# Two-layer hybrid block on one core: four reorderings inside the mixing stage and one at the end of the program

## The chip, the cores and the metric

One Trainium2 chip, one of its NeuronCores. The metric is device time in microseconds from launch to finish of one execution, median of several. The engines are named as in the profile: PE (TensorE) multiplies matrices, DVE (VectorE), ACT (ScalarE) and POOL (GpSimd) work element by element, SP issues DMAs. All inputs are float32 in HBM.

## The reference

Two layers over a 256 x 1024 activation `x`, each a feed-forward block, a mixing block with three branches, a cross attention to a memory and another feed-forward block:

```
for l in range(DEPTH):                                   # 2
    x = x + 0.5 * swiglu_ffn(rms_norm(x, ffn1_norm[l]), ffn1_w_gu[l], ffn1_w_down[l])
    h = rms_norm(x, mix_norm[l])
    (x_r, g_r, q_b, c_kv, q_i, k_i, w_i, q_c, k_c, v_c, f_c,
     gate_a, gate_b, gate_c) = jnp.split(h @ w_in[l], _split_points(), axis=-1)
    o_a = rglru_branch(...)      # convolution, two gates, a scan over time
    o_b = dsa_branch(...)        # 8 index heads score the keys, top 64 kept, softmax over them
    o_c = fox_branch(...)        # causal softmax with a forget bias
    merged = (sigmoid(gate_a) * (o_a @ w_branch[l, 0]) + sigmoid(gate_b) * (o_b @ w_branch[l, 1])
              + sigmoid(gate_c) * (o_c @ w_branch[l, 2]))
    x = x + merged @ w_out[l]
    x = x + memory_cross_attention(rms_norm(x, xattn_norm[l]), rms_norm(mem, mem_norm[l]), ...)
    x = x + 0.5 * swiglu_ffn(rms_norm(x, ffn2_norm[l]), ffn2_w_gu[l], ffn2_w_down[l])
return rms_norm(x, final_norm)
```

## The kernel before

**Weights.** Every weight comes through a ring of three SBUF slots in units of 1 MB (`raw`, 128 x 2048). To multiply in `float32r` without losing precision, ACT copies a unit, rounded, to `w_hi` in two halves (`split_hi`, L535) and DVE writes the rest `w_lo = raw - w_hi`, again in two halves (`split_lo`, L543). PE then forms three products per unit: hi x hi, hi x lo, lo x hi. A unit's split is written three units ahead of its use; the call is `splits(..., name)`, which splits the unit that takes the slot of `name`.

**Order.** There is no scheduler. Each engine's program is written out by hand, and engines wait for one another on semaphores that count: `job_done` (PE has finished a group), `bank_free[b]` (the result in bank b of `work` was taken away), `hi_ready`, `lo_ready`, `lg_ready`, `exp_ready`, `ri_ready`, `p_ready`. Class `Plan` walks through the units and groups in PE's order; `job` gives each group one of the four banks of `work` in turn, with two exceptions. A group may start only when the bank's previous group has been evacuated.

**The mixing stage** of a layer runs in this order on PE: normalized `x` through transposes (`nt`), units `xr0` to `gr1` of the first branch, the unit `misc` (whose result `nat` holds the key of the index, the latent `c` and the forget logits), the gates `rg` 0 and 1, transposes `fT` and `ki`, unit `qi0`, gates 2 and 3, transpose `cT`, unit `qi1`. Then the **index part**: eight small groups `("dots", i)`, with a unit after each second one (`qc0`, `kc0`, `qc1`, `kc1`). ACT takes relu of each (L1057), DVE sums them into `score` (`index_scores`). DVE does `index_scores(7)` only after the first logits.

Then the **stream**, 19 slots s with one unit each (`FILL`: `vc0`, `vc1`, `qb0`, `qb1`, `ga0`, ... `gc2` in slot 13, `gc3` 14, `bc1` 15, `gb0` 16). Softmax k (16 of them: 8 for the third branch, 8 for the second) passes through all engines: PE logits `("qk", k)` into `acc`; DVE scales and adds the bias into `lg[k % 2]` and takes the extreme (`nm`, `lg_ready`); ACT takes exp with sums (L1087, `exp_ready`); DVE the reciprocal (L1476, `ri_ready`); POOL multiplies (L797, `p_ready`); in slot k + 1 PE transposes the result (`("pt", k)`, L1920), and ACT copies it to `pt`. PE forms the logits 0 at the start of slot 0 and those of 2m - 1 and 2m at the start of odd slots.

DVE's program in a slot s is: logits of s; the first half of the split; reciprocal of s; `o_lo` of a finished pair; gating; the second half of the split; then, in slots 0 to 7, two of the sixteen top-8 rounds (two pairs of `max` and `match_replace`, L1496 and L1498) on `score`; in slots 13 to 16 the low part of two tiles of the normalized memory, `mem_lo` (`norm_lo`, L1184), which frees the bank of `("mt", s - 13)`. PE writes that bank with four transposes (L1938) just after the `pt` of the slot. The second branch's bias (`t5_score`, POOL) of softmax 8 to 11 needs the top 64 of rows 0 to 127 (rounds of slots 0 to 3), that of 12 to 15 those of rows 128 to 255 (slots 4 to 7).

**The end.** The last unit's product comes in four blocks of 128 x 512 (`LAST_BLOCKS`). For each DVE adds the block to `x` (`residual`, L1198) and multiplies by the final gain (L1205); ACT takes squares (L820), POOL the power -1/2 of the sums, and ACT and DVE each scale one half of a row block into `final_out`, which SP stores.

## Time and profile before

| | |
|---|---|
| runs | 1366.32 us median of 3 (1364.59 to 1366.35) |
| profiled execution | 1366.55 us, span 1364.7 us from first to last instruction |
| PE busy | 1344.5 us, 99% of the span |
| DVE busy | 951.2 us, 70% |
| ACT busy | 790.0 us, 58% |
| POOL busy | 133.8 us, 10% |
| granted clock of PE | 0.999 on average |

A timeline row gives the start, the duration and the number of like instructions in a row; in brackets stands the idle time of the engine before the row and what released it. PE's ends are modelled: groups that follow one another directly overlap a little by their rows, so that starts are the better measure there. The two layers repeat the same pattern some 674 us apart. The mixing stage lies at 195 to 500 us in layer 0 and at 869 to 1175 us in layer 1.

### The profile page before, as it was taken

Reading aid. Unit: us, or ns where it says so; the run is one execution under the profiler, and the core shown is the slowest. Engines: PE = TensorE matmul, PEld = TensorE weight load, DVE = VectorE, ACT = ScalarE, POOL = GpSimd, SP = SyncE. Lnnn points to the kernel's source line nnn. Section 1 sums busy time; section 2 is a strip of 40 time slices with the busy share of each in tenths; the row PEclk is TensorE's granted clock in tenths of the full one; section 3 lists DMA queues with packets and bytes.
Section 4 is the critical chain, followed back from the end, with each engine's and each line's share of the span. In section 5 each row is a group of like instructions: output and inputs, shape, how many; then the busy total and the mean of one; then the engine's idle time right before and its main releaser. Section 6 shows DMA issues by size and latency. Waiting matters only on the chain.

```text
span 1364.7 us, 23703 instructions
## 1 busy us (share of the span) xinstructions
PE 1344.5 (99%) x8805; PEld 1205.6 (88%) x8805; DVE 951.2 (70%) x1460; ACT 790.0 (58%) x1405; POOL 133.8 (10%) x168
## 2 busy tenths in 40 slices
PE   8999999999999999999999999999999999999997
PEld 7888889999999988888888888899999989888886
DVE  6666678888756667666676666789877656666665
ACT  7555566755744565555565555686566446655554
POOL 4010010022400110000010000101233001100000
PEclk9999999999999999999999999999999999999999
DMA  8687655655545447666566667555454555476661
GB/s 264 200 205 214 196 157 178 202 162 163 155 157 194 146 129 213 193 198 189 170 190 196 184 184 211 149 186 185 142 192 132 171 170 167 143 211 189 184 187 76
DMA packets 286385, 243.39 MB, mean 178 GB/s; under 512 B 14344, under 2 KB 263608, under 8 KB 286304
## 3 DMA queue, kind: packets, MB, share of 16 engines
q1 hardware_dynamic: 284176, 236.77, 57.1%
q10 hardware_dynamic: 1600, 4.25, 1.0%
q0 software_dynamic: 528, 1.26, 0.6%
q8 instruction: 54, 0.88, 0.3%
q14 instruction: 27, 0.22, 0.0%
HBM read 241.18 MB, written 1.27 MB: 178 GB/s over the span
## 4 chain that ended last, share of the span: by engine, by line
PE 60%; issue 24%; DVE 8%; ACT 4%; DVEq 3%; POOL 1%; POOLq 1%; ACTq 0%
PE work L1738 18%; PE acc L1695 16%; PE work L1666 12%; PE work L1742 9%; DVE w_lo L543 3%; PE work L1679 2%; ACT w_hi L535 1%; DVEq L1425 1%; PE acc L1591 1%; DVE score L1424 1%; ACT lg L1087 1%; POOL lg L797 1%; PE work L1908 1%; PE work L1920 1%; POOLq L742 0%
## 5 line engine op out<-in xcount | busy, mean ns | idle before, releaser
L543 DVE TENSOR_TENSOR w_lo<-raw,w_hi 128x1024 fp32r<-128x1024 f32 x444 | 543.1, 1244 | 89.7 <-ACT w_hi L535 87.9
L535 ACT ACTIVATE w_hi<-raw 128x1024 fp32r<-128x1024 f32 (+1 forms) x442 | 450.5, 1052 | 26.0 <-PE acc L1695 25.4
L1738 PE MATMUL work<-act,w_hi 128*128 128x512 f32 x1408 | 440.2, 394 | 0.0
L1742 PEld LDWEIGHTS work<-act,w_lo 128*128 128x128 f32 x1408 | 264.7, 188 | 60.2
L1742 PE MATMUL work<-act,w_lo 128*128 128x256 f32 x1408 | 277.7, 279 | 0.0
L1738 PEld LDWEIGHTS work<-act,w_hi 128*128 128x128 f32 x1408 | 214.7, 188 | 3.3 <-issue 0.2
L1666 PE MATMUL work<-act,w_hi 128*128 128x256 f32 x1536 | 197.9, 282 | 2.7 <-ACT act L995 1.1
L1666 PEld LDWEIGHTS work<-act,w_hi 128*128 128x128 f32 x1536 | 184.9, 188 | 8.0 <-issue 2.6
L851 ACT ACTIVATE gu_s<-work 128x256 f32<-128x256 f32 x176 | 57.8, 380 | 182.9 <-PE work L1742 182.9
L1219 DVE TENSOR_TENSOR gu_s<-gu_s,work 128x256 f32<-128x256 f32 x176 | 66.1, 417 | 121.7 <-ACT gu_s L851 121.3
L1695 PE MATMUL acc<-w_hi,h_lo 128*128 128x512 f32 x320 | 126.0, 394 | 0.0
L1695 PE MATMUL acc<-w_lo,h_hi 128*128 128x512 f32 x320 | 125.4, 392 | 0.0
L1695 PE MATMUL acc<-w_hi,h_hi 128*128 128x512 f32 x320 | 124.2, 388 | 0.0
L739 POOL TENSOR_SCALAR ms<-ssq 128x1 f32<-128x1 f32 x22 | 20.2, 916 | 883.8 <-ACT junk L820 883.1
L1666 PE MATMUL work<-act,w_lo 128*128 128x256 f32 x768 | 97.0, 278 | 0.0
L1666 PEld LDWEIGHTS work<-act,w_lo 128*128 128x128 f32 x768 | 92.3, 188 | 0.0
L861 ACT ACTIVATE h_hi<-h_f 128x256 fp32r<-128x256 f32 x80 | 33.4, 418 | 98.6 <-PE acc L1695 82.8
L1695 PEld LDWEIGHTS acc<-w_lo,h_hi 128*128 128x128 f32 x320 | 60.1, 188 | 12.3
L1695 PEld LDWEIGHTS acc<-w_hi,h_lo 128*128 128x128 f32 x320 | 60.2, 188 | 11.9
L1695 PEld LDWEIGHTS acc<-w_hi,h_hi 128*128 128x128 f32 x320 | 60.1, 188 | 11.8
L1238 DVE TENSOR_TENSOR h_lo<-h_f,h_hi 128x256 fp32r<-128x256 f32 x80 | 33.8, 422 | 45.7 <-ACT h_hi L861 45.7
L797 POOL TENSOR_TENSOR lg<-lg,ri 128x256 f32<-128x256 f32 (+1 forms) x32 | 39.1, 1222 | 195.1 <-DVE ri L1476 195.1
(247 smaller groups left out, 1541.7 us busy)
## 6 DMA issues: line engine op xcount, KB each, us to landing
raw<-in_ffn_w_gu SPq DMA_DIRECT2D x174, 512.0 KB, 5.0
raw<-in_w_in SPq DMA_DIRECT2D x52, 1024.0 KB, 5.2
raw<-in_ffn_w_down SPq DMA_DIRECT2D x44, 1024.0 KB, 4.9
raw<-in_w_branch SPq DMA_DIRECT2D x12, 1024.0 KB, 5.1
raw<-in_w_mkv SPq DMA_DIRECT2D x8, 1024.0 KB, 5.3
raw<-in_w_out SPq DMA_DIRECT2D x8, 1024.0 KB, 4.9
raw<-in_w_mq SPq DMA_DIRECT2D x4, 1024.0 KB, 5.4
raw<-in_w_mo SPq DMA_DIRECT2D x4, 1024.0 KB, 5.0
```

The lines of the kernel that those rows point to most:

```text
L535: eng.activation(halves(w_hi, slot, kind, part), halves(raw, slot, kind, part), ACT.Copy)\
L543: eng.tensor_tensor(halves(w_lo, slot, kind, part), halves(raw, slot, kind, part), halves(w_hi, slot, kind, part).bitcast(F32), ALU.subtra ...
L797: g.tensor_tensor(lg[:, s % 2, :, 0:s_len], lg[:, s % 2, :, 0:s_len], ri[:, s % 2, :].unsqueeze(2).to_broadcast([P, 2, s_len]), ALU.mult)\
L851: a.activation(gu_s[:, c, g, :], work[:, 2 * c + g, SEQ:2 * SEQ], ACT.Copy).then_inc(cross_ready, 1)
L861: a.activation(dst[:, c, :], h_f[:, c, :], ACT.Copy).then_inc(h_hi_ready, 1)
L1219: v.tensor_tensor(gu_s[:, c, g, :], gu_s[:, c, g, :], work[:, 2 * c + g, 0:SEQ], ALU.add)\
L1238: v.tensor_tensor(lo[:, c, :], h_f[:, c, :], hi[:, c, :].bitcast(F32), ALU.subtract)\
L1666: mm = pe.matmul(ps2(job)[:, m, :], ww[:, slot, first:first + P], xx[:, k, :], start=(n == 0 and k == 0 and m == 0), stop=(n == 2 and k == ...
L1679: mm = pe.matmul(out_ps(tt), xx[:, k, tt * P:tt * P + P], ww[:, slot, k * 256 + cols[0]:k * 256 + cols[1]], start=(n == 0 and k == 0 and t ...
L1695: mm = pe.matmul(acc[:, tt, nh * 512:nh * 512 + 512], xx[:, k0 + kk, tt * P:tt * P + P], ww[:, slot, kk * D + nh * 512:kk * D + nh * 512 + ...
L1738: pe.matmul(work[:, 2 * c + g, :], w_hi[:, slot, at_w:at_w + P], act[:, :, k, :], start=(k == 0), stop=False, skip_group_check=True)
L1742: mm = pe.matmul(work[:, 2 * c + g, 0:SEQ], w_lo[:, slot, at_w:at_w + P], act_hi[:, k, :], start=False, stop=(k == KT - 1), skip_group_che ...
```

## The change

1. **First norm of the mixing stage (DVE).** `scaled_rows(0)` and `(1)` (each scales a pair of transposed tiles in `acc`, 0.69 us) stand ahead of `scaled_xr(0)`.
2. **ACT before the index part.** The gates `rg` 0 ahead of the two squares of the latent, and the copy of `cT` ahead of the gates 2 and 3 and of the split `qi0`.
3. **First logits.** PE forms `("qk", 0)` ahead of the unit `kc1`, not behind it. ACT takes the first exp ahead of the copy of `kc1` and of the split that follows it. DVE takes the reciprocal ahead of that split's first half.
4. **Top-8 rounds.** Slots 0 to 5, 7 and 8 instead of 0 to 7: slot 6 has none.
5. **Banks.** `gc2` and `mt` 1 exchange banks 2 and 0; `mt` 3 and `gb0` exchange 0 and 1.
6. **`mem_lo`** ahead of the second half of the split in slots 13 to 16.
7. **The end.** DVE adds block 3 to `x` straight after block 2, before it multiplies block 2 by the gain and scales row block 0. ACT takes all four squares before it scales row block 0.

```diff
+TOP_SLOTS = (0, 1, 2, 3, 4, 5, 7, 8)
+SWAPPED = {("bc1", 1): 1, ("pt", 15): 3, "gc2": 2, ("mt", 1): 2, ("mt", 3): 1, "gb0": 3}
...
-            if name in (("bc1", 1), ("pt", 15)):
-                bank = (bank + (1 if name[0] == "bc1" else 3)) % 4
+            bank = (bank + SWAPPED.get(name, 0)) % 4
...
                 wait_done(a, l, "nat")
...
+                rg_gates(0)
                 a.drain()
                 for tt in range(TT):
                     a.activation(c_nat[:, tt, :], nat[:, tt, HD + HEADS:F_AT], ACT.Square,
                                  accum_out=ssq[:, tt, 0:1]).then_inc(ssq_ready, 1)
-                rg_gates(0)
...
+                copy_out(l, "cT", c_t[:], ps("cT")[:, 0:SEQ])
                 rg_gates(2)
                 rg_gates(3)
...
                 splits(a, split_hi, l, "qi0")
-                copy_out(l, "cT", c_t[:], ps("cT")[:, 0:SEQ])
...
+                    if i == IDX_SLOTS - 1:
+                        exponential(0)
                     if i in IDX_FILL:
                         filler(l, IDX_FILL[i])
                         splits(a, split_hi, l, IDX_FILL[i])
...
-            squares(DEPTH, 0, range(3))
+            squares(DEPTH, 0)
             for tt in range(TT):
-                if tt == 1:
-                    squares(DEPTH, 0, (3,))
...
-                scaled_xr(0)
                 scaled_rows(0)
                 scaled_rows(1)
+                scaled_xr(0)
...
                     if s == 0:
                         index_scores(IDX_SLOTS - 1)
+                        reciprocals(s)
                     ahead = FILL[s - 1] if s else IDX_FILL[IDX_SLOTS - 1]
                     splits(v, split_lo, l, ahead, (0,))
...
                     filler(l, FILL[s], (0,))
+                    if 13 <= s < 17:
+                        for k in (2 * (s - 13), 2 * (s - 13) + 1):
+                            norm_lo(l, 4, k, mem_hi, mem_lo, ("mt", k // 2), 3)
                     splits(v, split_lo, l, ahead, (1,))
...
-                    if s < 8:
+                    if s in TOP_SLOTS:
+                        at_s = TOP_SLOTS.index(s)
...
+                    for b in range(2):
+                        residual(l, 3, None, (b,))
+                        gained_block(b)
+                    residual(l, 3, None, (2, 3))
                     final_scale(0)
-                    residual(l, 3, None, (3,))
+                    gained_block(2)
+                    gained_block(3)
                     final_scale(1)
...
                     mm.then_inc(job_done, 1)
+                    if i == IDX_SLOTS - 1:
+                        qk(0)
                     if i in IDX_FILL:
                         filler(l, IDX_FILL[i])
```

**ACT at the border of index part and stream.** The rows begin with the relu of `dots` 7; `lg,sm<-lg,nm` is the first exp, `kc<-work` the copy of `kc1`, `w_hi<-raw` the split behind it. Before:

```order
L1057 ACTIVATE lg<-work 128x512 [waits score_step,job_done]
L844 ACTIVATE kc<-work 128x512 [waits job_done]
L535 ACTIVATE w_hi<-raw 128x1024 [waits job_done,landed1]
L535 ACTIVATE w_hi<-raw 128x1024
L1087 ACT_TABLE_LOAD
L1087 ACTIVATE lg,sm<-lg,nm 128x128 [waits lg_ready]
L1087 ACTIVATE lg,sm<-lg,nm 128x128
```

Now:

```order
L1069 ACTIVATE lg<-work 128x512 [waits score_step,job_done]
L1059 ACT_TABLE_LOAD
L1059 ACTIVATE lg,sm<-lg,nm 128x128 [waits lg_ready]
L1059 ACTIVATE lg,sm<-lg,nm 128x128
L847 ACTIVATE kc<-work 128x512 [waits job_done]
L538 ACTIVATE w_hi<-raw 128x1024 [waits job_done,landed1]
L538 ACTIVATE w_hi<-raw 128x1024
```

The table load and the two exps have moved over the copy and the split, which now stand behind a wait for `lg_ready`.

**DVE at the end of slot 6 and in slot 7.** The first row is the second gating of `ba0` (`merged<-gate,work`), which ends slot 6 but for the rounds; `lg<-acc,fox_bias` is the logits of slot 7, and what follows it belongs to that slot. Before:

```order
L1291 SCALAR_TENSOR_TENSOR merged<-gate,work 128x512 [waits bank_free0,job_done]
L1496 MAX top_134<-score 128x8
L1498 MATCH_REPLACE score<-top_134,score 128x256
L1496 MAX top_134<-score 128x8
L1498 MATCH_REPLACE score<-top_134,score 128x256
L1457 SCALAR_TENSOR_TENSOR lg<-acc,fox_bias 128x512 [waits causal_ready,job_done]
L1469 TENSOR_REDUCE nm<-lg 128x2
L543 TENSOR_TENSOR w_lo<-raw,w_hi 128x1024 [waits hi_ready]
L1476 RECIPROCAL ri<-sm 128x2 [waits exp_ready]
```

Now:

```order
L1292 SCALAR_TENSOR_TENSOR merged<-gate,work 128x512 [waits bank_free0,job_done]
L1462 SCALAR_TENSOR_TENSOR lg<-acc,fox_bias 128x512 [waits causal_ready,job_done]
L1474 TENSOR_REDUCE nm<-lg 128x2
L546 TENSOR_TENSOR w_lo<-raw,w_hi 128x1024 [waits hi_ready]
L1449 RECIPROCAL ri<-sm 128x2 [waits exp_ready]
L1487 TENSOR_TENSOR o_lo_72<-work,o_hi_71 128x2x128 [waits o_part]
L546 TENSOR_TENSOR w_lo<-raw,w_hi 128x1024 [waits hi_ready]
L1505 MAX top_134<-score 128x8
L1507 MATCH_REPLACE score<-top_134,score 128x256
```

The four rows of rounds between slot 6 and slot 7 are gone. Slot 7 keeps its rounds, and the last four rows of rounds now stand in slot 8.

**DVE in slot 15.** `gate<-gate,work` and `merged<-merged,gate` are the first gating of `bc1`, `mem_lo` the low part of memory tiles 4 and 5. Before:

```order
L1295 SCALAR_TENSOR_TENSOR gate<-gate,work 128x512 [waits bank_free2,job_done]
L1298 TENSOR_TENSOR merged<-merged,gate 128x512
L543 TENSOR_TENSOR w_lo<-raw,w_hi 128x1024 [waits hi_ready]
L1184 SCALAR_TENSOR_TENSOR mem_lo<-work,gain,mem_hi 128x256 [waits act_hi_ready]
L1184 SCALAR_TENSOR_TENSOR mem_lo<-work,gain,mem_hi 128x256
L1295 SCALAR_TENSOR_TENSOR gate<-gate,work 128x512 [waits bank_free1,job_done]
L1298 TENSOR_TENSOR merged<-merged,gate 128x512
```

Now:

```order
L1296 SCALAR_TENSOR_TENSOR gate<-gate,work 128x512 [waits bank_free0,job_done]
L1299 TENSOR_TENSOR merged<-merged,gate 128x512
L1191 SCALAR_TENSOR_TENSOR mem_lo<-work,gain,mem_hi 128x256 [waits act_hi_ready]
L1191 SCALAR_TENSOR_TENSOR mem_lo<-work,gain,mem_hi 128x256
L546 TENSOR_TENSOR w_lo<-raw,w_hi 128x1024 [waits hi_ready]
L1296 SCALAR_TENSOR_TENSOR gate<-gate,work 128x512 [waits bank_free1,job_done]
L1299 TENSOR_TENSOR merged<-merged,gate 128x512
```

`mem_lo` and the half split have changed places; the bank that the gate row waits for is 0 instead of 2.

## Rows read from the trace of the kernel before

**Rows 1.** Page, section 1: busy us (share of the span) x instructions.
```profile
PE 1344.5 (99%) x8805; PEld 1205.6 (88%) x8805; DVE 951.2 (70%) x1460; ACT 790.0 (58%) x1405; POOL 133.8 (10%) x168
```

**Rows 2.** Waits of PE: line, waited for; us in total, times, longest.
```profile
PE work L1920 <- POOL lg L797: 3.1, 4, 0.8
PE work L1938 <- DVE mem_lo L1184: 1.9, 2, 0.9
PE work L1666 <- ACT act L995: 1.1, 2, 0.5
PE work L1666 <- ACT c_t L844: 0.9, 2, 0.6
```

**Rows 3.** Windows: us; busy PE, PEld, DVE, ACT, POOL; PEclk, DMA, GB/s.
```profile
241.30:278.90 37.60, 36.40 (x311) 34.27 (x310) 34.30 (x55) 27.32 (x41) 3.03 (x2) 1.00 0.64 199
1357.50:1361.00 3.50, 0.00 (x0) 0.00 (x0) 2.20 (x5) 1.67 (x6) 0.86 (x2) 1.00 0.39 150
```

**Rows 4.** Timeline, DVE, slot 0: start, duration in us, engine, line, operation.
```profile
272.01 0.42 DVE L1469 TENSOR_REDUCE nm<-lg 128x2 f32<-128x256 f32 x1
274.05 1.23 DVE L543 TENSOR_TENSOR w_lo<-raw,w_hi 128x1024 fp32r<-128x1024 f32 x1 [0.17 <-issue]
...
275.27 1.21 DVE L543 TENSOR_TENSOR w_lo<-raw,w_hi 128x1024 fp32r<-128x1024 f32 x1
```

**Rows 5.** Timeline, ACT, slot 0, layer 0.
```profile
269.79 2.00 ACT L535 ACTIVATE w_hi<-raw 128x1024 fp32r<-128x1024 f32 x2
271.80 1.28 ACT L1087 ACT_TABLE_LOAD   x1
273.10 0.40 ACT L1087 ACTIVATE lg<-lg,nm 128x128 f32<-128x128 f32 x1
```

**Rows 6.** Timeline, POOL and PE, slots 1, 2; brackets: idle, releaser.
```profile
280.80 1.51 POOL L797 TENSOR_TENSOR lg<-lg,ri 128x256 f32<-128x256 f32 x1 [3.85 <-DVE ri L1476]
...
277.00 0.44 PE L1920 MATMUL work<-ident,lg 128*128 128x128 f32 x2 [0.83 <-POOL lg L797]
...
282.93 0.38 PE L1920 MATMUL work<-ident,lg 128*128 128x128 f32 x2
```

**Rows 7.** Timeline, DVE, ACT and PE, slots 6 to 8, layer 0.
```profile
320.14 0.41 DVE L1496 MAX8 top<-score 128x8 f32<-128x256 f32 x1
...
322.32 0.69 DVE L1457 SCALAR_TENSOR_TENSOR lg<-acc,fox_bias 128x512 f32<-128x512 f32 x1
...
323.81 0.51 ACT L1087 ACTIVATE lg<-lg,nm 128x256 f32<-128x256 f32 x1 [1.19 <-DVE nm L1469]
...
321.75 1.98 PE L1666 MATMUL work<-act,w_lo 128*128 128x256 f32 x16
323.57 1.98 PE L1666 MATMUL work<-act,w_hi 128*128 128x256 f32 x16
326.28 0.66 PE L1920 MATMUL work<-ident,lg 128*128 128x128 f32 x4 [0.74 <-POOL lg L797]
```

**Rows 8.** Timeline, slot 13 (ACT, PE) and 16 (DVE, PE), layer 0.
```profile
362.74 0.60 ACT L844 ACTIVATE pt<-work 128x512 f32<-128x512 f32 x1 [0.19 <-PE work L1920]
...
363.33 0.74 PE L1666 MATMUL work<-act,w_hi 128*128 128x256 f32 x4 [0.20 <-DVE gate L1295]
...
384.30 0.87 DVE L1184 SCALAR_TENSOR_TENSOR mem_lo<-work,gain,mem_hi 128x256 fp32r<-128x256 f32 x2
...
385.31 0.63 PE L1938 MATMUL work<-ident,mem_x 128*128 128x128 f32 x4 [0.94 <-DVE mem_lo L1184]
```

**Rows 9.** Timeline, PE and DVE, end of the program.
```profile
1356.99 0.40 PE L1695 MATMUL acc<-w_hi,last_lo 128*128 128x512 f32 x1
...
1358.22 0.74 DVE L1198 SCALAR_TENSOR_TENSOR x<-acc,scaled_rstd,x 128x512 f32<-128x512 f32 x1
```

**Rows 10.** Timeline, PE, start of the program.
```profile
3.69 2.61 PE L1801 MATMUL work<-ident 128*128 128x128 f32 x11 [3.69 <-POOLq L733]
...
9.80 1.91 PE L1801 MATMUL work<-ident 128*128 128x128 f32 x16
```

More of the change, by code:

```diff
@@ L1050, in _, with exponential @@
                 splits(a, split_hi, l, "qi1")
+                def exponential(s):
+                    s_len = P * ((s % 8) // 4 + 1)
+                    a.wait_ge(lg_ready, l * STREAM + s + 1)
+                    for j in range(2):
+                        e = a.activation(lg[:, s % 2, j, 0:s_len], lg[:, s % 2, j, 0:s_len], ACT.Exp, scale=-1.0,
+                                         bias=nm[:, s % 2, j:j + 1], accum_out=sm[:, s % 2, j:j + 1])
+                    e.then_inc(exp_ready, 1)
                 for i in range(IDX_SLOTS):
@@ L1082, in _ @@
                         splits(a, split_hi, l, FILL[s - 1])
-                    if s < STREAM:
-                        s_len = P * ((s % 8) // 4 + 1)
-                        a.wait_ge(lg_ready, l * STREAM + s + 1)
-                        for j in range(2):
-                            e = a.activation(lg[:, s % 2, j, 0:s_len], lg[:, s % 2, j, 0:s_len], ACT.Exp, scale=-1.0,
-                                             bias=nm[:, s % 2, j:j + 1], accum_out=sm[:, s % 2, j:j + 1])
-                        e.then_inc(exp_ready, 1)
+                    if 0 < s < STREAM:
+                        exponential(s)
                     if s in (2, 3):
@@ L1444, in _, with reciprocals @@
                         splits(v, split_lo, l, IDX_FILL[i])
+                def reciprocals(s):
+                    v.wait_ge(exp_ready, l * STREAM + s + 1)
+                    v.reciprocal(ri[:, s % 2, :], sm[:, s % 2, :]).then_inc(ri_ready, 1)
                 for s in range(STREAM + 3):
@@ L1499, in _ @@
                             v.drain()
-                        if s % 4 == 3:
+                        if at_s % 4 == 3:
                             v.tensor_scalar(sc, sc, 0.5 * TAKEN, NEG, ALU.is_gt, ALU.mult).then_inc(score_ready, 1)
-                    if 13 <= s < 17:
-                        for k in (2 * (s - 13), 2 * (s - 13) + 1):
-                            norm_lo(l, 4, k, mem_hi, mem_lo, ("mt", k // 2), 3)
                     if s != 6:
@@ L1574, in final_scale, with gained_block @@
                                         ALU.mult).then_inc(out_ready[1], 1)
-                    residual(l, 3, None, range(3))
+                    def gained_block(b):
+                        tt, nh = LAST_BLOCKS[b]
+                        cols = slice(nh * 512, nh * 512 + 512)
+                        if b == 0:
+                            v.wait_ge(final_gain_landed, 16)
+                        v.drain()
+                        v.tensor_tensor(final_out[:, tt, cols], x[:, tt, cols], final_gain[:, cols], ALU.mult)\
+                         .then_inc(gained, 1)
+                    for b in range(2):
+                        residual(l, 3, None, (b,))
+                        gained_block(b)
+                    residual(l, 3, None, (2, 3))
                     final_scale(0)
-                    residual(l, 3, None, (3,))
+                    gained_block(2)
+                    gained_block(3)
                     final_scale(1)
@@ L1833, in _, with qk @@
                 late_transposes(l, 1, params)
+                def qk(k):
+                    blk, pr = slot_of(k)
+                    s_len = P * (blk + 1)
+                    queries, keys = (qc, kc) if k < 8 else (qb, k_b)
+                    wait_jobs(pe, l, [f"qc{pr // 2}", f"kc{pr // 2}"] if k < 8 else [f"qb{pr // 2}", ("kb", pr // 2)])
+                    if k >= 2:
+                        pe.wait_ge(lg_ready, l * STREAM + k - 1)
+                    for j in range(2):
+                        mm = pe.matmul(logits(k)[:, j, :], queries[HD * j:HD * j + HD, pr, blk * P:blk * P + P],
+                                       keys[HD * j:HD * j + HD, pr, 0:s_len], start=True, stop=True)
+                    mm.then_inc(job_done, 1)
                 def rg_gates(m):
@@ L1889, in _ @@
                     for k in qk_slots(s):
-                        blk, pr = slot_of(k)
-                        s_len = P * (blk + 1)
-                        queries, keys = (qc, kc) if k < 8 else (qb, k_b)
-                        wait_jobs(pe, l, [f"qc{pr // 2}", f"kc{pr // 2}"] if k < 8 else [f"qb{pr // 2}", ("kb", pr // 2)])
-                        if k >= 2:
-                            pe.wait_ge(lg_ready, l * STREAM + k - 1)
-                        for j in range(2):
-                            mm = pe.matmul(logits(k)[:, j, :], queries[HD * j:HD * j + HD, pr, blk * P:blk * P + P],
-                                           keys[HD * j:HD * j + HD, pr, 0:s_len], start=True, stop=True)
-                        mm.then_inc(job_done, 1)
+                        qk(k)
                     if pv_pair(s) is not None:
```

17 lines of the change are left out of this document (6 added, 11 removed).

## Prediction

> **What bounds the kernel now.** I read the page's busy shares first. PE is busy 1344.5 of 1364.7 us [rows 1], so that no reordering can win more than the 20 us in which it isn't, start and end of the program included. The second view is what PE waits for. It holds all that this change can reach: transposes of a softmax waiting for POOL's multiplication, 3.1 us in four waits; the memory transposes waiting for DVE's `mem_lo`, 1.9 us in two; projection units waiting for ACT, 1.1 and 0.9 us in four [rows 2]. Each occurs once or twice a layer. The third view, windows, shows who stands behind these waits. From 241.3 to 278.9 us, the index part up to slot 1, DVE is busy 34.30 of 37.60 us with 55 groups [rows 3]; the 3.3 us left are 0.06 us apiece, the drains between dependent operations. DVE waits for nobody there. That stretch, and not PE, sets when the first softmaxes are done, and the reader should keep it in mind: PE time that is won ahead of it can be lost at its end.
>
> **Part 1 and 2, before the index part.** The waits for `act` (0.55 us a layer) and for `c_t` (0.45) mostly go, since ACT gets its first scaled tiles one DVE piece sooner and copies `cT` before two gates. DVE itself gains at most the few tenths that it waited there for ACT, and ACT hands as much back with the copy, about 0.4 us, that now stands in front of the gates 2 and 3, which release DVE's long stretch. So DVE's stretch begins when it did, within 0.1 us. PE arrives about 1 us sooner at the end of the index part. Value of its own: nothing, if PE is then made to wait for the same DVE stretch (next part).
>
> **Part 3, first logits.** Moving PE's four matmuls costs nothing. What counts is the queue on ACT. DVE reaches `nm` of softmax 0 at 272.01 + 0.42 = 272.43 [rows 4] as before, because DVE and not PE was late there. ACT has had its table load (1.28 us) by then; before, too, it ran at 271.80, ahead of `nm` [rows 5]. The two exps take some 0.9 us (0.40 each and the readouts [rows 5]) and end at 273.4. DVE's reciprocal follows at 274.05, where the half split stood [rows 4], and not at 275.2. Even with 1.51 us for the multiplication [rows 6] `p_ready` comes at 275.8 and not at 276.95: the stall of 0.83 us at 277.00 [rows 6] goes.
>
> But the copy of `kc1` and its split now stand behind ACT's wait. Copy 273.4 to 273.9 (0.60 us for this shape [rows 8], starts overlap by 0.1), first half split to 274.95, second to 275.9 (2.00 us the two [rows 5]). DVE, which took these halves at 274.05 and 275.27 and ended at 276.48 [rows 4], can take the first at 275.0 to 276.2 and the second to 277.3. It is 0.85 us later, and it has no reserve: rounds, logits 1, split and reciprocal follow on one another. POOL's multiplication of softmax 1 ends not at 280.80 + 1.51 = 282.31 but at 283.16, and PE transposes it at 283.2, not at 282.93 [rows 6]. So PE, 1.8 us ahead (0.83 + about 1), waits some 2.1 us in slot 2 and leaves it **0.27 us later than before**. Bounds: below, -1.83 us a layer, if nothing of this holds PE (0.83 + 0.55 + 0.45); above, +1.55, if the table load starts only with `nm` (0.27 + 1.28). I take +0.27, since the rows of slot 0 carry each step. Two layers: **+0.5 us** (-3.7 to +3.1).
>
> **Part 4, rounds.** In slot 7 PE stands 0.74 us before the transposes at 326.28. By starts it is more: the groups at 321.75 and 323.57 are 1.82 apart, so that the next was due at 325.39, 0.89 before [rows 7]. The two rounds of slot 6 fill 320.14 to 322.32, when the logits of slot 7 begin [rows 7]. Without them DVE is 2.1 us sooner, but ACT's exp can use only the 1.19 us that it stood idle (323.81 [rows 7]); its splits come first. 1.15 against 0.89: the stall goes, with 0.25 us to spare. The rounds themselves, 2.2 us, lie in slot 8, where PE has no wait and DVE has the 2.1 us in hand that it got in slot 6. Bounds: 0 to -0.89; the margin would be gone if the multiplication took 0.25 longer, and POOL's spans vary by more than that. I take all: **-1.8 us** for two layers.
>
> **Parts 5 and 6, banks and `mem_lo`.** In slot 16 the transposes `mt` 3 stand 0.94 us, by starts 1.0, until `mem_lo` of `mt` 2 is through at 384.30 + 0.87 [rows 8]. Now `mt` 3 goes to bank 1, which the gating of `bc1` freed before 383, and `mem_lo` is a half split earlier; `gb0`, in bank 0, needs that `mem_lo` only by 384.6, when it is done at 384.1. The wait goes: **-2.0 us** for two layers (bounds 0 and -2.1). In slot 13 `gc2` waited 0.20 us for DVE's gating, to 363.33. In bank 0 it waits for ACT's copy of `pt` 12, 362.74 + 0.60 = 363.34 [rows 8]: no gain. The split halves that fall behind `mem_lo` are needed two slots later.
>
> **Part 7, the end.** PE's last product ends at 1356.99 + 0.40 = 1357.39, and DVE takes it up at 1358.22 [rows 9], 0.8 us late, because it first multiplies block 2 by the gain and scales. Squares, sums, power and last scaling hang on it one after the other. They start 0.8 us sooner; DVE's own queue behind it, two gain products and two scalings, is nearly as long as that chain and takes 0.1 back: **-0.7 us** (0 to -0.8).
>
> **Sum.** +0.5 - 1.8 - 2.0 - 0.7 = -4.0 us; with the rounding of part 3 (0.54) and part 4 (1.78), -3.9. From the profiled execution's 1366.55 that gives 1362.65; the median of the runs is 0.23 lower, so 1362.4.
>
> **Rivals.** (a) *DVE doesn't hold slot 2.* Then parts 1 to 3 give their 1.83 us a layer instead of costing 0.27: 4.2 us more, 1358.2. For it: ACT stands idle there, and its order can matter in ways that rows of the other order don't show. Against it: DVE's 34.30 of 37.60 us.
>
> (b) *ACT comes later still, or slot 7 keeps its wait.* If the table load waits with the exp, DVE loses 1.28 us more in each layer: 1365.0. The same if POOL's multiplication in slot 7 eats the margin (1.8 us back: 1364.2). Against it: the load at 271.80 ran before its operand was there.
>
> (c) *The exchange moves the wait and doesn't remove it.* In bank 2 the pair product of slot 15 now follows `mt` 1, and needs its `mem_lo` earlier than `mt` 2 did. If `mem_lo` of slot 14 were 1 us late there, the 2.0 us would stay: 1364.4. Against it: it no longer stands behind a half split.
>
> (d) *Slower.* The 2.1 us hole in slot 2 is over twice as long as any stall that PE has now. If it made the granted clock fall to the lower of its levels, 1.2 instead of 2.4 GHz, matmuls would run at half pace for a while. The start shows that pace: 11 transposes in 2.61 us at 3.69, 16 in 1.91 at 9.80, and at most 6.1 us between the two [rows 10]. Half of 6.1 in each layer is 6.1 us more: 1368.5. It decides at the hole's length. Against it: after the last matmul PE was idle from 1357.50 to 1361.00 with the granted clock at 1.00 [rows 3], 3.5 us, more than the hole. The Trainium skill (TensorE: Matmul & The Clock Gate, Part 1) says that the gate grants by how busy PE has been recently and that the throttled state is the default; by that rule a hole can cost a stretch at half rate, and the trace agrees only that the clock does fall some time after the work ends, later than this hole would last.
>
> **Chances and range.** Forecast 0.66, (a) 0.08, (b) 0.14, (c) 0.09, (d) 0.03. The range goes from inside (a) to (b), 1358.8 to 1365.2: it leaves out (d) and the far halves of (a) and (b). A measurement of this kernel tells 0.2%, 2.7 us, from no change; the forecast lies 1.2 us beyond that. Faster 0.70: the forecast but for a tenth of its cases, and (a). Same 0.26: (b), (c) and that tenth. Slower 0.04.
>
> **What the profile will show.** Right: PE's waits for `mem_lo` gone; no wait at the first softmax transposes of a stream, and one of about 2 us at the second; none in slot 7; the DVE half split of slot 0 begun near 275 us and waiting for ACT's `w_hi`; last residual 0.04 us after the last matmul. Wrong: stream slot 2 ends sooner than before relative to the layer's start (a); table load after `nm`, or a wait in slot 7 (b); a wait of the pair product on `mem_lo` in slot 15 (c); a granted clock under 1.00 inside the mixing stage (d).

## The result, and the profile after

| | before | after |
|---|---|---|
| median of 5 runs | 1366.06 us (1364.59 to 1366.35) | 1358.49 us (1357.65 to 1359.28) |
| span of the profiled execution | 1364.7 us | 1356.7 us |
| PE busy | 1344.5 us | 1338.8 us |

The ratio is 0.9946 (95% interval 0.9935 to 0.9957): 7.6 us faster, where 3.9 us were forecast. The time lies 0.3 us under the range.

The busy times from the page of after answer [rows 1]:

```profile
PE 1338.8 (99%) x8805; PEld 1202.2 (89%) x8805; DVE 953.3 (70%) x1460; ACT 789.4 (58%) x1405; POOL 127.8 (9%) x168
```

PE executes the same 8805 matmuls and is busy 5.7 us less. About half of that is how busy time is counted: a matmul in front of a wait counts with its modelled end, some 0.28 us, and with 0.11 us where the next one follows directly, so that waits and small matmuls that go or change places take 2.7 us of busy time with them. The other 2.9 us lie between 256-column matmuls that follow one another directly in both kernels. No term of the sum had a place for those.

The waits of PE in after answer [rows 2] (columns: line, waited for; us in total, times, longest):

```profile
PE work L1944 <- POOL lg L800: 4.4, 4, 1.9
PE work L1685 <- ACT pt L847: 0.5, 2, 0.2
PE work L1757 <- DVE w_lo L546: 0.4, 1, 0.4
```

The waits for `mem_lo`, `act`, `c_t` and `gate` are gone. That for POOL's multiplication has grown from 3.1 to 4.4 us: it went from the first softmax of a stream, where 0.33 us are left, to the second. On PE's timeline, layer 0, after, answering [rows 6]:

```profile
274.30 0.44 PE L1944 MATMUL work<-ident,lg 128*128 128x128 f32 x2 [0.33 <-POOL lg L800]
...
278.35 2.05 PE L1698 MATMUL work<-w_hi,act 128*128 128x256 f32 x16
282.29 0.44 PE L1944 MATMUL work<-ident,lg 128*128 128x128 f32 x2 [1.90 <-POOL lg L800]
```

The hole in slot 2 is there, 1.90 us by this view and 2.06 by starts, where 2.1 was forecast.

**Where PE's time went.** I set the start of each matmul in the trace of after against its counterpart of before. The last one starts 7.94 us sooner. The rest of the program, up to the end, is 0.09 us shorter.

| place | forecast, both layers | traces |
|---|---|---|
| start of the program | 0 | -0.15 |
| up to slot 2 (parts 1 to 3) | +0.54 | -0.63 (-0.49 and -0.14) |
| slot 7 (part 4) | -1.78 | -1.79 |
| slot 16 (parts 5, 6) | -2.0 | -2.27 |
| matmuls that follow one another faster | none | -3.1 (what is left) |
| after the last matmul (part 7) | -0.7 | -0.09 |
| sum | -3.9 | -8.0 |

The second line holds some pace of its own, 0.2 us gained in layer 0 and 0.3 us lost in layer 1. By waits and order alone the two layers are alike there, -0.30 and -0.43. The expectations below give 0.54 and 0.20 us for this line; matmul by matmul it is 0.49 and 0.14. "Slot 7" is the prediction's name: it goes by softmax 7, whose transposes PE does in slot 8.

**The pace.** The fifth line can be read off the timeline. Here a row is a group of 16 matmuls, and the difference of two starts is the time of 16. Before, in the first units behind slot 16:

```profile
394.34 2.05 PE L1666 MATMUL work<-act,w_lo 128*128 128x256 f32 x16
396.23 2.05 PE L1666 MATMUL work<-act,w_hi 128*128 128x256 f32 x16
...
409.42 2.05 PE L1666 MATMUL work<-act,w_hi 128*128 128x256 f32 x16
411.30 2.05 PE L1666 MATMUL work<-act,w_lo 128*128 128x256 f32 x16
```

After, the same groups:

```profile
391.85 1.98 PE L1685 MATMUL work<-act,w_lo 128*128 128x256 f32 x16
393.66 1.98 PE L1685 MATMUL work<-act,w_hi 128*128 128x256 f32 x16
...
406.35 1.98 PE L1685 MATMUL work<-act,w_hi 128*128 128x256 f32 x16
408.17 1.98 PE L1685 MATMUL work<-act,w_lo 128*128 128x256 f32 x16
```

1.88 to 1.89 us for 16 became 1.81 to 1.82. In start times of single matmuls: 256-column matmuls in a row start either every 113.3 ns or every 117.9 to 118.0 ns, and hardly ever anything between. They settle on one of the two within about five matmuls of a new start (a transpose, a pair product, a wait) and keep it to the next one. Before, 2638 intervals are slow and 2318 fast; after, 1977 and 2984. 661 fewer slow ones, 4.7 ns each, are 3.1 us. The longest stretch without a new start is behind the pair product of slot 17, a run of 286 intervals, 390 to 423 us. It was slow in both layers before and is fast in both after. The runs behind it, up to 463 us, gain 0.6 us more. From the start of that run to the end of the query projections before takes 74.75 us and after 72.85: 1.9 us in each layer. The granted clock is 1.00 in all of it, in both kernels. It is neither the clock nor a wait, and the view of waits doesn't show it.

### The profile page after: what moved, and what is told of

The parts are those of the page before. It is cut to its first block, busy times and chain, and to the rows that moved or that the text cites. A ratio compares the mean times of both kernels' runs of the same rounds, so it can differ in the third digit from the quotient of the medians.

```text
span 1356.7 us, 23703 instructions
## 1 busy us (share of the span) xinstructions
PE 1338.8 (99%) x8805; PEld 1202.2 (89%) x8805; DVE 953.3 (70%) x1460; ACT 789.4 (58%) x1405; POOL 127.8 (9%) x168
## 4 chain that ended last, share of the span: by engine, by line
PE 65%; issue 22%; DVE 6%; ACT 3%; DVEq 2%; POOLq 1%; POOL 1%; ACTq 0%
PE work L1757 18%; PE work L1685 16%; PE acc L1714 16%; PE work L1761 9%; DVE w_lo L546 2%; PE work L1944 1%; PE acc L1862 1%; PE work L1932 1%; PE work L1698 1%; DVEq L1426 1%; DVE score L1425 1%; PE acc L1610 1%; ACT w_hi L538 1%; POOLq L745 0%; DVE xc L1360 0%
## 5 line engine op out<-in xcount | busy, mean ns | idle before, releaser
L800 POOL TENSOR_TENSOR lg<-lg,ri 128x256 f32<-128x256 f32 (+1 forms) x32 | 35.5, 1110 | 199.2 <-DVE ri L1449 199.2
```

Of the source, the lines that this page charges most:

```text
L800: g.tensor_tensor(lg[:, s % 2, :, 0:s_len], lg[:, s % 2, :, 0:s_len], ri[:, s % 2, :].unsqueeze(2).to_broadcast([P, 2, s_len]), ALU.mult)\
```

## Experiments

Fourteen kernels beside the two. "Run of 286" is that stretch; "S" is 118 ns, "F" 113 ns, layer 0 and then layer 1. The second column of letters is the unit of slot 16, just ahead of it. Ratios are to before, on the same chip. (Some expectations give times such as 401 or 476 us: those are on the trace's own clock, 11.1 us ahead of the profile's.)

| kernel | median (range), us | ratio, 95% interval | slot 16 | run of 286 |
|---|---|---|---|---|
| before | 1365.5 to 1366.2 | | F F | S S |
| after | 1358.49 (1357.65 to 1359.28) | 0.9946 [0.9935, 0.9957] | S S | F F |
| e1_banks | 1360.32 (1359.76 to 1360.79) | 0.9960 [0.9946, 0.9973] | S S | F F |
| e2_late_logits | 1359.04 (1358.92 to 1360.21) | 0.9950 [0.9936, 0.9963] | S S | F F |
| e3_tail | 1359.10 (1357.48 to 1359.83) | 0.9947 [0.9933, 0.9961] | S S | F F |
| e4_probe | 1364.39 (1363.16 to 1366.30) | 0.9990 [0.9981, 0.9999] | S F | F S |
| e5_before | 1365.95, one run | | F F | S S |
| e6_rounds | 1354.85 (1354.34 to 1355.11) | 0.9926 [0.9913, 0.9940] | S S | F F |
| e7_tail_gain | 1358.92 (1357.91 to 1359.62) | 0.9955 [0.9941, 0.9969] | S S | F F |
| e8_probe2 | 1363.32 (1362.32 to 1364.54) | 0.9987 [0.9978, 0.9997] | F S | F F |
| e9_rounds_late | 1357.09 (1356.78 to 1357.26) | 0.9940 [0.9927, 0.9953] | S S | F F |
| e10_best | 1354.52 (1354.08 to 1354.94) | 0.9922 [0.9910, 0.9935] | S S | F F |
| e11_parts123 | 1367.07 (1362.32 to 1368.73) | 1.0008 [0.9999, 1.0016] | F F | S S |
| e12_after | 1359.66 (1358.29 to 1360.19) | 0.9959 [0.9946, 0.9972] | S S | F F |
| e13_memlo | 1361.54 (1359.87 to 1363.96) | 0.9970 [0.9961, 0.9980] | F F | S S |
| e14_swap | 1364.18 (1361.88 to 1365.67) | 0.9991 [0.9982, 1.0000] | F S | S F |

### What sets the pace

**e1_banks** puts parts 5 and 6 alone into before.

```diff
-            if name in (("bc1", 1), ("pt", 15)):
-                bank = (bank + (1 if name[0] == "bc1" else 3)) % 4
+            bank = (bank + SWAPPED.get(name, 0)) % 4
...
                     filler(l, FILL[s], (0,))
+                    if 13 <= s < 17:
+                        (norm_lo of two tiles)
                     splits(v, split_lo, l, ahead, (1,))
```

> Kernel before with parts 5 and 6 alone (bank exchange, mem_lo ahead of the second half split). Theory W (the time that PE waits is all there is): the two waits for mem_lo go, 1.1 us each, so -2.2 us against before. Theory P (between 401 and 476 us of layer 0, and in layer 1, 256-column matmuls start 117.9 ns apart in before and 113.3 in after, 286 of them in one run and some 190 behind it; the pace is chosen where PE starts again after a break): removing the stall in slot 16 shifts the next starts, and the pace behind it may change with it: -2.2 and up to -3.4 more, -5.6 us. If the pace stays at 117.9 there, the faster pace of after comes from the earlier parts.

Measured: -5.9 us, theory P. These two parts alone bring more than the whole forecast of -3.9; 2.3 us of it is the wait, the rest pace. In the trace 0.7 us of that pace lie ahead of slot 16, where the edit changes nothing. Parts 1 to 4 and 7 together add only 1.8 us (0.7 by e12_after, the repetition of after).

**e4_probe** and **e8_probe2** put one small matmul in front of the run.

```diff
+                            if s == 17 and k == 2 * n:
+                                cut = (16, 64)[l]          # e8_probe2: (64, 16)
+                                pe.matmul(pv_ps(n)[0:HD, 0, 0:cut], values[:, 0, ...], pt[:, 0, 0, 0, 0:cut],
+                                          start=True, stop=True)
```

> Kernel before with one more small matmul (64 x 64, 16 columns in layer 0 and 64 columns in layer 1, its result overwritten by the next) ahead of the pair product of slot 17, just before the run of 286 matmuls at 117.9 ns. If the pace is chosen by the moment at which PE starts the run, at least one layer may show 113.3 ns behind it, -1.6 us for a layer; if it hangs on the operands or banks of these units, both stay at 117.9 and the time at before's within 0.3 us.

> As e4_probe with the two layers exchanged: the added matmul ahead of the pair product of slot 17 has 64 columns in layer 0 and 16 in layer 1. In e4_probe 16 columns turned the run of 286 to 113.3 ns and 64 columns did not. If the length of the delay decides, layer 0 now stays at 117.9 and layer 1 turns to 113.3. If the layer or chance decides, the pattern does not cross over.

Both came out faster than before, with three of four long runs fast. But the two didn't cross over: 64 columns stayed slow in e4_probe and turned fast in e8_probe2. And the table's letters for slot 16 show that in two of the three fast cases the unit of slot 16, ahead of the added matmul, had already taken the other pace than in before. There the added matmul is not what turned the run. So the probes say that the operands and banks of the run don't fix its pace; which delay gives which pace they don't say. By the medians they gain 1.8 and 2.6 us.

**e5_before** is before, once more.

> The kernel before, unchanged, profiled once more. If the pace of the 256-column matmuls is a matter of this program's own timing, the run of 286 behind slot 17 starts every 117.9 ns again in both layers, and some 2640 of 4956 such matmuls in all. If it is chance from one execution to the next, the pattern differs and one of the two long runs may come at 113.3.

Slow in both layers again, 2727 slow intervals against 2638. The long runs repeat; single shorter units differ between the two executions.

**e13_memlo** is part 6 alone, **e14_swap** part 5 alone.

> The kernel before with part 6 alone: mem_lo ahead of the second half split, all banks as before. By the trace of before mem_lo of mt 2 ends about 1.2 us sooner, near the moment at which mt 3 is due, so the wait of 1.1 us a layer in slot 16 shrinks to 0.2 or nothing. Theory S (the stall sets the pace behind it): with the stall gone the slot 16 unit starts every 117.9 ns and the run of 286 every 113.3, as in e1_banks, and the time is e1_banks's 1360.3 within 1 us. Theory B (the banks set the pace): the run stays at 117.9 and the time is 1363.5 to 1364.

> The kernel before with part 5 alone, the exchange of banks; mem_lo stays behind the second half split. The transposes mt 3 go to bank 1 and don't wait, but gb0, now in bank 0, waits for the mem_lo of mt 2, and the pair product of slot 15 for that of mt 1. Theory B: the run of 286 comes at 113.3 ns in both layers. Theory S: where PE still starts again on DVE's mem_lo ahead of the slot 16 unit or at it, the pace is not the one of the kernels without stall, and can be 117.9. Time by the waits alone: gb0 is due about 0.5 us after mt 3 was, so half of the wait remains, 1364.9; with the run at 113.3 it would be 1361.

In e13_memlo the wait is gone, 1.1 us a layer, with the banks of before, and the run is slow in both layers of the profiled execution: theory S fails in the form in which I gave it. That execution was the slowest of nine, 1363.96 us. The others go down to 1359.87, which is what the same kernel would take with both runs fast (1.9 us each); the pace there was not seen, only the times. The start times of the matmuls around the transposes `mt` 3 show what is different, in ns between one start and the next, layer 0:

```
                 pt -> mt   mt      unit of slot 16                         its pace
before             1217   136 109   207 118 114 113 113 114 113 113         113
e13_memlo           110   116 109   207 118 113 114 113 113 114 113         113
e1_banks            109   109 109   200 118 117 119 117 118 118 118         118
after               109   110 109   201 118 117 118 118 117 119 117         118
```

In e13_memlo a trace of the wait may be left: the first transpose takes 6 to 7 ns longer to the next one. In nine kernels with parts 5 and 6 (after, e1, e2, e3, e6, e7, e9, e10, e12), 18 layers, these gaps are 109 to 110 ns; the unit is slow and the run behind it fast 18 times in 18. In the four with the banks of before and no added matmul (before, e5, e11 with a wait of 1.1 us, e13 with the 6 ns), the unit is fast and the run slow 8 times in 8. The kernels with a probe or with a wait elsewhere (e4, e8, e14) are mixed. In 31 of all 32 layers the two letters are opposite.

In e14_swap the two layers have the same banks, and one ran slow and one fast; e4_probe and e8_probe2 ran fast with the banks of before. So the banks alone don't set the pace: theory B is out. The waits of e14_swap are at `gb0`, as expected, 0.61 and 0.41 us, and eat half of what the exchange brings; part 5 needs part 6. What the traces show is that the choice is made at a new start and held to the next, and that the letters of the unit and of the run behind it are opposite in 31 of 32 layers. The reading that fits this is that each unit takes its pace from the moment at which PE starts again, and that it hands on the state. It is not shown as a cause: e13_memlo and e1_banks differ by 6 ns and by the banks of part 5, so that no pair of kernels here differs in the moment alone.

The times agree in part. The kernels without a wait at slot 16 and without the hole of slot 2 (e1, e2, e6, e9, e10) spread over 0.5 to 1.3 us in five runs each, and before over 1.8 in its five; before spreads over 2.3 to 3.6 in sets of 15 to 19 runs, and e13_memlo over 4.1 in nine. What in PE holds two intervals, and what moment gives which, stays open.

### Slot 2, and parts 1 to 3

**e11_parts123** has parts 1, 2 and 3 alone.

> The kernel before with parts 1, 2 and 3 alone. The prediction's sum says +0.27 us a layer, +0.5 us. The traces of before and after say that PE reaches the second softmax transposes 0.54 us (layer 0) and 0.20 us (layer 1) sooner relative to the start: -0.7 us. Rival (a) of the prediction (PE isn't held in slot 2): -3.7 us. Pace: the run of 286 stays at 117.9 ns, since the stall in slot 16 is still there. The hole of 1.9 us in slot 2 may bring the granted clock down for some 3.5 us, 1.3 us each time.

1.6 us slower by the medians, 1.1 by the ratio, whose interval just includes no change: nearer to the forecast's +0.5 than to -0.7. Two things lie in it. Against the layer's start PE reaches the second softmax 0.5 and 0.2 us sooner, not later, as in after. But behind the hole the profiled execution loses 1.5 us in layer 0 against before. The windows there (columns: us; busy PE, PEld, DVE, ACT, POOL; PEclk, DMA, GB/s):

```profile
280.00:283.00 3.00, 1.11 (x9) 0.88 (x8) 2.66 (x7) 1.19 (x6) 2.12 (x2) 1.00 0.41 144
283.00:284.00 1.00, 1.00 (x7) 0.92 (x6) 0.84 (x4) 1.00 (x2) 0.08 (x1) 0.85 0.46 109
284.00:285.00 1.00, 1.00 (x7) 1.00 (x7) 0.85 (x4) 1.00 (x2) 0.00 (x0) 0.50 1.04 403
285.00:286.00 1.00, 1.00 (x6) 1.00 (x6) 1.00 (x2) 1.00 (x6) 0.00 (x0) 0.50 1.05 401
286.00:287.00 1.00, 1.00 (x7) 1.00 (x6) 1.00 (x3) 0.44 (x1) 0.67 (x1) 0.50 0.44 154
287.00:288.00 1.00, 1.00 (x10) 1.00 (x10) 0.93 (x4) 0.00 (x0) 1.00 (x2) 0.94 0.02 6
```

The granted clock is at its lower level, 1.2 GHz, for 3.4 us, from about 1.3 us after PE took up work again at 282.45. Its matmuls start every 213 ns there. That is rival (d), at 1.5 us in one layer where I had priced 3.05. It comes and goes: five traces have the hole (after, e3, e7, e11, e12), ten layers, and the clock fell in three of them. In the eleven other traces, with no wait of PE over 1.3 us in the mixing stage, it fell in none of 22 layers. The times of the other runs go with it. In after, e12, e3 and e7 the ten runs with a mean granted clock of 0.999 took 1357.48 to 1358.70 us, and the ten with 0.997 or 0.998 took 1358.92 to 1360.19. The 6.4 us over which e11_parts123 spreads are more than this accounts for; its fastest run, 1362.32 us, and its profiled one, 1367.12 us, both have 0.998.

**e2_late_logits** undoes parts 2 and 3 in after.

> The changed kernel with parts 2 and 3 undone (ACT order before the index part, first logits); parts 1, 4, 5, 6, 7 stay. By the prediction's sum, +0.27 us a layer for parts 1 to 3, this kernel would be about 0.5 us faster than the changed one. By the traces of before and after (PE at the second softmax transposes 0.54 and 0.20 us earlier relative to the layer's start) it is 0.7 us slower. Anything beyond 1 us must be pace: the number of 256-column matmuls at 117.9 instead of 113.3 ns tells.

1359.04 against 1358.49 and 1359.66 for after and its repetition: parts 2 and 3 are worth nothing that can be measured, in after. Behind the start of the program the traces give them 0.25 us in both layers together. PE's waits in it are 0.8 us in slot 1 again and none in slot 2.

**e6_rounds** moves the top-8 rounds out of slot 0.

```diff
-TOP_SLOTS = (0, 1, 2, 3, 4, 5, 7, 8)
+TOP_SLOTS = (1, 2, 3, 4, 5, 7, 8, 9)
```

> The changed kernel with the top-8 rounds in slots 1 to 5 and 7 to 9: none in slot 0. They stood between the split of kc1 and the logits of softmax 1 (276.43 to 278.0 in layer 0) and so in the chain that PE waits for in slot 2, 1.90 us by the waits and 2.06 by starts. Theory: that wait shrinks by the 1.5 us of the rounds to about 0.5 us, -1.5 us a layer, -3.0 us against the changed kernel, about 1355.5. Rival: the rounds are late next in slot 9 or in softmax 8's bias, or the wait just moves to slot 3: no gain. With the shorter hole the granted clock should stay at 1.00 behind it.

1354.85 us, 11.0 under before. The wait in slot 2 is 0.30 us, and PE gains 1.61 and 1.45 us there. PE's timeline of e6_rounds at the place shown above for after:

```profile
274.39 0.44 PE L1944 MATMUL work<-ident,lg 128*128 128x128 f32 x2 [0.33 <-POOL lg L800]
...
278.44 2.04 PE L1698 MATMUL work<-w_hi,act 128*128 128x256 f32 x16
280.79 0.44 PE L1944 MATMUL work<-ident,lg 128*128 128x128 f32 x2 [0.30 <-POOL lg L800]
```

DVE takes the logits of softmax 1 at 276.52, straight behind the split, instead of 278.02. With the hole the falls of the clock are gone from the trace as well, and five runs lie within 0.8 us.

**e9_rounds_late** is that without parts 2 and 3.

> e6_rounds with parts 2 and 3 undone (first logits, ACT order), the rounds still in slots 1 to 5 and 7 to 9. Theory (parts 2 and 3 bring PE forward by 1.4 to 2 us a layer, which the changed kernel gives back whole in slot 2 because DVE's chain through the rounds ends no sooner; the two belong together): without them moving the rounds gains nothing, PE waits in slot 1 (0.8 us) and not in slot 2, and the time is that of e2_late_logits, 1358 to 1359, that is 3 to 4 us above e6_rounds. Rival (the rounds in slot 0 were the cost all along, parts 2 and 3 are worth nothing): the time stays within 1 us of e6_rounds.

1357.09, 2.2 us above e6_rounds: between the two, and nearer to the theory. In the traces the two parts are worth 1.2 us a layer here and 0.1 in after. The rounds' move without them brings nothing by waits (slot 2 had no wait, slot 1 keeps its 0.83); e9_rounds_late is faster than e2_late_logits all the same, 1.95 us by the medians of two sets on two chips. Behind the start the traces differ by 1.5 us, of which 1.1 lie in the pace ahead of slot 0, where the two are the same program, and 0.3 at the transposes of softmax 5, in slot 6. So parts 2 and 3 need the move of the rounds; what the move gives without them is not told apart from pace.

### After the last matmul

**e3_tail** and **e7_tail_gain** change DVE's order at the end of after.

```diff
 e3_tail                                      e7_tail_gain
-for b in range(2):                          -for b in range(2):
+for b in range(3):                          +for b in range(4):
     residual(l, 3, None, (b,))                   residual(l, 3, None, (b,))
     gained_block(b)                              gained_block(b)
-residual(l, 3, None, (2, 3))                -residual(l, 3, None, (2, 3))
+residual(l, 3, None, (3,))                   final_scale(0)
 final_scale(0)                              -gained_block(2)
-gained_block(2)                             -gained_block(3)
 gained_block(3)                              final_scale(1)
 final_scale(1)
```

> The changed kernel, but at the end the gain product of block 2 stands ahead of the residual of block 3, in the 0.48 us in which DVE waits for PE; the row block scaling and the product of block 3 stay behind the residual. Theory C (POOL's two operations took 0.68 and 0.89 us instead of 0.30 and 0.56 because DVE's two gain products ran at the same time): residual 0.35 us later, POOL back to 0.30 and 0.56 and 0.7 us sooner, net -0.3 us. Rival (the chain of POOL is slower for another reason): +0.35 us.

> The changed kernel with each block's gain product straight behind its residual and both scalings of DVE at the end. The gain product of block 3 then ends (about 1352.7 on the time scale of e3_tail's trace) before POOL begins its two operations. Theory C (DVE's tensor_tensor beside them makes POOL's two operations longer): they take 0.30 and 0.56 us again and the end comes about 0.4 us sooner than in e3_tail and 0.5 sooner than in the changed kernel. Rival (the scaling of row block 0, now beside POOL, slows it just as well): no difference.

The end of after, DVE and POOL on the timeline (answering [rows 9]):

```profile
1349.48 0.75 DVE L1205 SCALAR_TENSOR_TENSOR x<-acc,scaled_rstd,x 128x512 f32<-128x512 f32 x1 [0.48 <-PE acc L1714]
1350.33 0.49 DVE L1579 TENSOR_SCALAR final_out<-final_out,rstd 128x512 f32<-128x512 f32 x1
1350.91 1.48 DVE L1588 TENSOR_TENSOR final_out<-x,final_gain 128x512 f32<-128x512 f32 x2
1352.84 0.48 DVE L1579 TENSOR_SCALAR final_out<-final_out,rstd 128x512 f32<-128x512 f32 x1 [0.45 <-POOL rstd L746]
...
1351.09 0.68 POOL L742 TENSOR_SCALAR ms<-ssq 128x1 f32<-128x1 f32 x1 [1.66 <-ACT junk L823]
1351.91 0.89 POOL L746 TENSOR_TENSOR rstd<-ms,minus_half 128x1 f32<-128x1 f32 x1
```

And POOL at the end of before:

```profile
1359.82 0.30 POOL L739 TENSOR_SCALAR ms<-ssq 128x1 f32<-128x1 f32 x1 [2.46 <-ACT junk L820]
1360.27 0.56 POOL L743 TENSOR_TENSOR rstd<-ms,minus_half 128x1 f32<-128x1 f32 x1
```

POOL's two operations on 128 x 1 took 0.86 us before and take 1.57 in after, where they start while DVE multiplies. Here is POOL in e3_tail, where the first starts beside one gain product and the second beside nothing:

```profile
1352.74 0.68 POOL L742 TENSOR_SCALAR ms<-ssq 128x1 f32<-128x1 f32 x1 [1.88 <-ACT junk L823]
1353.56 0.56 POOL L746 TENSOR_TENSOR rstd<-ms,minus_half 128x1 f32<-128x1 f32 x1
```

And in e7_tail_gain, where the first starts beside DVE's scaling and the second beside nothing:

```profile
1352.61 0.58 POOL L742 TENSOR_SCALAR ms<-ssq 128x1 f32<-128x1 f32 x1 [1.88 <-ACT junk L823]
1353.34 0.56 POOL L746 TENSOR_TENSOR rstd<-ms,minus_half 128x1 f32<-128x1 f32 x1
```

So theory C holds for both kinds of DVE operation, and e7's rival in part. It doesn't hold for every kind. For row block 0 the first of the two starts beside DVE's residual, which reads `acc`, and takes 0.30 us in all sixteen traces:

```profile
1356.20 0.74 DVE L1198 SCALAR_TENSOR_TENSOR x<-acc,scaled_rstd,x 128x512 f32<-128x512 f32 x1
1356.35 0.30 POOL L739 TENSOR_SCALAR ms<-ssq 128x1 f32<-128x1 f32 x1 [175.16 <-ACT junk L820]
```

Both gains are smaller than expected, 0.12 us in the trace of e3_tail and 0.22 in that of e7_tail_gain against 0.3 and 0.5: the first operation got none or little of its time back, and the last residual starts 0.23 us later. From the start of the last matmul to the last scaling: before 3.88, after 3.79, e3_tail 3.67, e7_tail_gain 3.57. The medians of the last two don't show it; both have the hole of slot 2, and in their traces a fall of the clock in one of two layers: layer 1 in e3_tail, layer 0 in e7_tail_gain.

**e12_after** is the repetition of after.

> The changed kernel again, on the chip of the three others. 1358.5 us; the run of 286 at 113.3 ns in both layers, as in all six kernels with the bank exchange so far; the granted clock down behind the hole in slot 2 in none, one or both layers (in the three kernels that have this hole it was down in two of six layers).

1359.66 us, both long runs fast, no fall of the clock in the profiled execution, and a spread of 1.9 us.

**e10_best** joins e6_rounds and the end of e7_tail_gain.

> e6_rounds with the end of e7_tail_gain. In e7_tail_gain's trace the last residual began 0.65 us after PE's last matmul began and the last scaling 2.92 us behind it, together 3.57, against 0.43 + 3.36 = 3.79 in the changed kernel: -0.2 us, so 1354.6. Rival: the same as e6_rounds within its runs, 1354.3 to 1355.1.

1354.52 us, ratio to before 0.9922 (0.9910 to 0.9935), the fastest of all. Its 3.57 us from the last matmul to the last scaling stand against 3.79 in e6_rounds, as expected; the medians differ by 0.33 us, with overlapping ranges.

## Why the prediction was wrong

**A term was missing.** The step that failed is the sum itself: it counted waits, and it put the time between two matmuls that wait for nothing at no change, without a reason. Of the 4.1 us that the traces moved beyond the forecast, about 3 are in that time. The mark was there: in before the groups of 16 in [rows 7] start 1.82 us apart and those behind slot 16 1.89, and I read only gaps. No rival had it either.

**Up to slot 2: the hole was right, its moment wrong.** Forecast: DVE's stretch "begins when it did, within 0.1 us", and PE leaves slot 2 0.27 us later. Traces: 0.49 and 0.14 us sooner. DVE, after:

```profile
240.73 1.14 DVE L1404 TENSOR_SCALAR rg_r<-rg_r,ch 128x256 f32<-128x256 f32 x4 [1.74 <-ACT rg_i L1011]
...
273.39 0.17 DVE L1449 RECIPROCAL ri<-sm 128x2 f32<-128x2 f32 x1 [0.17 <-issue]
274.15 2.36 DVE L546 TENSOR_TENSOR w_lo<-raw,w_hi 128x1024 fp32r<-128x1024 f32 x2 [0.59 <-ACT w_hi L538]
...
280.49 0.16 DVE L1449 RECIPROCAL ri<-sm 128x2 f32<-128x2 f32 x1
```

The stretch begins at 240.73 and not at 241.39: 0.66 us sooner. The copy of `cT` did stand on ACT for 0.37 us ahead of the gates, as forecast. But the chain ahead of it, DVE's convolution and the splits behind it, came 0.93 us sooner (`f_z` at 229.81 instead of 230.74), where I had allowed "a few tenths". I looked at what ACT gave DVE in the first norm and not at what else stood on DVE between there and `f_z`. From there on the steps hold, shifted by that 0.66 and by another 0.25 that the steps on ACT and DVE took less than reckoned. DVE stands 0.59 us for the split of `kc1`, and the reciprocal of softmax 1 comes at 280.49. POOL's first multiplication ends at 274.24, and PE, which the sum had waiting for nothing there, still stands 0.33 us. The table load ran, and then ACT stood 2.9 us for the operand; rival (b) had nothing.

**Slot 7: right**, -1.79 against -1.78, though the rounds went to the very slot 8 of which the prediction says that PE has no wait there: its wait, that of softmax 7's transposes, is the one that this part takes away. No run has part 4 alone. **Slot 16: right**, -2.27 against -2.0, and rival (c) is out: the pair product waits for no `mem_lo`.

**The end: wrong.** The residual does start 0.8 us sooner against the last matmul (0.43 us behind it, not 1.23). I moved the products under POOL's two operations and took POOL's time from the rows in which DVE was idle beside them. They took 0.71 us more, and of 0.7 us 0.09 are left.

**Rivals.** (a), with 0.08, gives 1358.2 and so the measured time, and it is wrong: its mechanism is that PE isn't held in slot 2, and PE stands there 1.90 us. A time that fits doesn't prove a mechanism. (d) had 0.03, and its mechanism is real though its time was not: the hole does bring the clock down, in three of ten layers, but in neither layer of the profiled execution of after. I had argued against it with the 3.5 us of idle PE at the end at clock 1.00 [rows 3]. That row shows what the clock does in a pause; here it fell when the pause was over and PE had been at work again for 0.8 to 1.3 us. The price was wrong too, half of 6.1 us; it is 3.4 us at half pace, of which the traces show 1.5 to 1.6 as lost. The rule that I cited says that the gate grants by how busy PE has been recently (the Trainium skill, TensorE: Matmul & The Clock Gate, Part 1). The three falls behind the hole agree with it; why the other seven holes of the same length brought none, no run shows.

**The chances.** They don't add up as they are worded. The forecast but for a tenth of its cases and (a) make 0.67 for faster, and (b), (c) and that tenth make 0.30 for the same, not 0.70 and 0.26.

## What to carry to other kernels

Where PE is busy 99% of the time, compare the start times of its matmuls in both traces and not only its waits: the same matmuls can follow one another 4% slower for tens of us, and an edit ahead of them can turn that. In the nine kernels in which no other engine releases PE at slot 16 the long run was fast 18 times in 18. In the four with the banks of before and DVE's `mem_lo` just ahead of PE it was slow 8 times in 8, and with an added matmul or a wait a little further on it came out either way. If an edit brings the bounding engine forward, follow the next engine's queue to the place where the two meet and clear it there in the same edit: parts 2 and 3 were worth nothing measurable in after and 2.2 us with the rounds moved.

## What the runs showed of the hardware

- Matmuls of 256 columns with a weight load each start 113.3 or 117.9 ns apart at a granted clock of 1.00. The state is taken within about five matmuls of a new start and held for up to 286; it changed with edits that left these matmuls, their operands and their banks as they were (e4_probe, e8_probe2, layer 0: fast in both, slow in before).
- After a pause of PE of 2.1 us by starts the granted clock went to 0.50 for 3.4 us in three of ten cases, beginning 0.8 to 1.3 us after PE was back at work. In the eleven kernels whose pauses are at most 1.3 us it fell in none of 22 layers.
- How long a POOL operation on 128 x 1 elements takes depends on the DVE operation beside which it starts. The scaling of the sums (`ms`) takes 0.30 us with DVE idle and 0.30 beside a residual that reads `acc`, 0.58 beside DVE's last scaling, 0.68 beside a gain product and 1.94 beside a half split (the middle one of 205 in the sixteen traces). The same was seen at the multiplication of softmax 0: 1.51 us in before, beside a half split, and 0.61 in after, where DVE stood.
- A table load of ACT took 1.28 us in all sixteen cases in before and all sixteen in after, and the one ahead of the first exp ran before the wait of that exp.
